# Joined products in two more gate units of the first attention and two more units of the second

## The reference

```python
def first_block(x, ...):
    xn = rmsnorm(x, norm_attn[l])
    proj = xn @ w_in[l]
    rq, rk, rv, rg, sq, sk, sv, ga, gb = jnp.split(proj, split_points, axis=-1)
    ...                                             # retention over rq, rk, rv
    ret = ret.astype(x.dtype) * jax.nn.silu(rg)
    y_a = ret @ w_branch_ret[l]
    ...                                             # stick-breaking attention over sq, sk, sv
    y_b = sb @ w_branch_sb[l]
    mixed = jax.nn.sigmoid(ga) * y_a + jax.nn.sigmoid(gb) * y_b
    x = x + mixed @ w_out[l]
    ...                                             # experts: every one of 16384, gated by a top 16

def second_block(x, ...):
    xn = rmsnorm_2(h, norm1_g[layer])
    proj = xn @ w_in[layer]
    q_a, k_a, v_a, q_r, f_r, i_r, g_r = jnp.split(proj, IN_SPLITS, axis=-1)
    attn = moba_attention(q_a, k_a, v_a)            # at 256 tokens: causal softmax with a distance term
    rec = hgrn2(q_r, f_r, i_r, g_r, lb_all[layer], rec_norm_g[layer])
    h = h + jnp.concatenate([attn, rec], axis=-1) @ w_out[layer]
    ...                                             # experts again
```

## Time and profile before

| | us |
|---|---|
| median of 3 runs | 1983.34 (1983.23 to 1983.45) |
| profiled execution, its own time | 1983.32 |
| its span | 1981.5 |
| PE busy | 1973.2 |
| DVE, ACT, POOL busy | 1282.0, 1043.9, 1424.8 |

### The profile page before, as it was taken

How to read it: one execution, slowest core, us unless ns; L and a number is a source line. 1 busy time by engine, 2 the same in 40 slices (tenths; PEclk the granted TensorE clock), 3 DMA queues, 4 the chain that set the end, 5 groups by cost and what they waited for, 6 DMA issues and landing times.

```text
span 1981.5 us, 38996 instructions
## 1 busy us (share of the span) xinstructions
PE 1973.2 (100%) x13942; PEld 1763.5 (89%) x13942; DVE 1282.0 (65%) x2183; ACT 1043.9 (53%) x1364; POOL 1424.8 (72%) x604
## 2 busy tenths in 40 slices
PE   9999999999999999999999999999999999999998
PEld 8899898888888888888889899888888888888887
DVE  5256387864776899953336748886467789994333
ACT  6556555565555544445447665556555554444444
POOL 7667878888777878854448757888877787884442
PEclk9999999999999999999999999999999999999999
DMA  8444545555555555566555345555555555555553
GB/s 271 163 139 149 178 162 186 189 183 189 179 170 174 176 169 171 174 209 206 194 188 180 124 143 170 191 188 185 181 178 169 174 176 170 175 174 180 201 191 127
DMA packets 100467, 351.44 MB, mean 177 GB/s; under 512 B 12464, under 2 KB 15408, under 8 KB 100272
## 3 DMA queue, kind: packets, MB, share of 16 engines
q1 hardware_dynamic: 99680, 348.61, 52.9%
q10 hardware_dynamic: 720, 1.92, 0.3%
HBM read 349.44 MB, written 1.05 MB: 177 GB/s over the span
## 4 chain that ended last, share of the span: by engine, by line
PE 99%; DMA 0%; DVE 0%; ACT 0%; POOL 0%; SPq 0%; issue 0%
PE ps L1268 24%; PE ps L1334 12%; PE ps L1269 12%; PE ps L1336 12%; PE ps L1337 6%; PE ps L1335 6%; PE ps L739 4%; PE ps L741 4%; PE ps L740 4%; PE ps L896 4%; PE ps L1260 3%; PE ps L898 2%; PE ps L933 1%; PE ps L823 1%; PE ps L1244 1%; PE ps L1146 1%
## 5 line engine op out<-in xcount | busy, mean ns | idle before, releaser
L657 POOL TENSOR_TENSOR wlo<-ring,whi 128x1024 fp32r<-128x1024 f32 x565 | 1370.3, 2431 | 515.0 <-ACT whi L1694 427.7
L1694 ACT ACTIVATE whi<-ring 128x1024 fp32r<-128x1024 f32 x536 | 566.6, 1060 | 718.2 <-PE ps L1337 387.2
L1268 PE MATMUL ps<-hboth,whi 128*128 128x512 f32 x2048 | 714.6, 395 | 0.0
L1269 PE MATMUL ps<-hboth,wlo 128*128 128x256 f32 x2048 | 567.7, 277 | 0.0
L1268 PEld LDWEIGHTS ps<-hboth,whi 128*128 128x128 f32 x2048 | 384.1, 188 | 87.3
L1334 PE MATMUL ps<-whi,shi 128*128 128x512 f32 x1024 | 404.2, 395 | 0.0
L1336 PE MATMUL ps<-wlo,shi 128*128 128x512 f32 x1024 | 400.4, 391 | 0.0
L1269 PEld LDWEIGHTS ps<-hboth,wlo 128*128 128x128 f32 x2048 | 384.6, 188 | 0.0
L1337 PE MATMUL ps<-whi,slo 128*128 128x256 f32 x1024 | 286.7, 280 | 0.0
L1335 PE MATMUL ps<-whi,slo 128*128 128x256 f32 x1024 | 285.7, 279 | 0.0
L1336 PEld LDWEIGHTS ps<-wlo,shi 128*128 128x128 f32 x1024 | 192.2, 188 | 43.4
(11 more groups left out here) (335 smaller groups left out, 2893.7 us busy)
## 6 DMA issues: line engine op xcount, KB each, us to landing
ring<-in_weights SPq DMA_DIRECT2D x651, 512.0 KB, 3.3
act<-in_const SPq DMA_DIRECT2D x11, 198.0 KB, 3.5
act<-in_const SPq DMA_DIRECT2D x8, 192.0 KB, 4.9
xres<-in_x SPq DMA_DIRECT2D x4, 256.0 KB, 5.2
act<-in_keys ACTq DMA_DIRECT2D x1, 1024.0 KB, 4.7
ring<-in_weights SPq DMA_DIRECT2D x2, 256.0 KB, 5.0
act<-in_fgain ACTq DMA_DIRECT2D x1, 512.0 KB, 3.5
out<-act SPq DMA_DIRECT2D x1, 512.0 KB, 2.6
```

Source lines behind the costliest of these rows:

```text
L657: pool.tensor_tensor(wlo[:, j, :], ring[:, j, :], whi[:, j, :].bitcast(F32), ALU.subtract)\
L1268: pe.matmul(bank(b), whi[:, j, c], hboth[:, :, kc, :], start=kc == 0, stop=False, skip_group_check=True)
L1269: mm = pe.matmul(bank(b, 0, S), wlo[:, j, c], hhi[:, kc, :], start=False, stop=kc == KC - 1, skip_group_check=True)
L1694: eng.activation(whi[:, j, :], ring[:, j, :], ACT.Copy).then_inc(hi_ready[j], 1)
```

## The change

Four units change from `columns` to `joined_columns`: units 24 and 25 of the first attention (the last half of ga) and units 4 and 5 of the second (the first halves of qa and ka). Units 24 and 25 now use banks 2, 3 and 0, 1. Before these are written PE waits until the stick-breaking steps have read them (`stay_ready`, `arg_ready`). Units 4 and 5 use banks 4, 5 and 0, 1. The slots, the transfers and POOL's work stay as they are.

```diff
+JOINED_GATE_BANK = {24: 2, 25: 0}
...
-JOINED2_BANK = {1: 6, 2: 4, 3: 6}
+JOINED2_BANK = {1: 6, 2: 4, 3: 6, 4: 4, 5: 0}
...
+        gate_part = tmpA[:, :, 0:S]
...
-            def joined_columns(i, b, free, left=None):
+            def joined_columns(i, b, free, left=None, parts=(0, 1)):
...
-                for half in range(HALVES):
+                for half in parts:
...
+                        elif i in JOINED_GATE_BANK:
+                            free = (stay_ready, PAIRS) if i == 24 else (arg_ready, PAIRS)
+                            joined_columns(HALVES * i, JOINED_GATE_BANK[i], [free] * TT, parts=parts)
...
+                        if i in JOINED_GATE_BANK:
+                            b = JOINED_GATE_BANK[i]
+                            if i > 24:
+                                eng.wait_ge(gate_joined, i - 24)
+                            eng.activation(gate_part, ps[:, b:b + 2, S:2 * S], ACT.Copy).then_inc(gate_parted, 1)
...
-                        eng.wait_ge(slot_used, HALVES * (i + 1))
-                        eng.tensor_tensor(gateT[name][:, off // P:off // P + 2, :], bank(4 + i % 2).rearrange("p (j t) -> p j t", j=2),
-                                          R, ALU.mult).then_inc(gate_scaled, 1)
+                        if i in JOINED_GATE_BANK:
+                            b = JOINED_GATE_BANK[i]
+                            product = ps[:, b:b + 2, 0:S]
+                            eng.wait_ge(gate_parted, i - 23)
+                            eng.tensor_tensor(product, product, gate_part, ALU.add).then_inc(gate_joined, 1)
+                            eng.wait_ge(gate_joined, i - 23)
+                        else:
+                            product = bank(4 + i % 2).rearrange("p (j t) -> p j t", j=2)
+                            eng.wait_ge(slot_used, HALVES * (i + 1))
+                        eng.tensor_tensor(gateT[name][:, off // P:off // P + 2, :], product, R, ALU.mult).then_inc(gate_scaled, 1)
```

More of the change, by code:

```diff
@@ L478, in block_program @@
         so_copied = sem("sb_out_copied")
+        gate_parted = sem("gate_low_part_copied")
+        gate_joined = sem("gate_parts_joined")
         ret_parted = sem("ret_low_part_copied")
```

## The result

The changed kernel takes 1988.86 us in the median of 9 runs (1986.96 to 1990.8), the kernel before beside it 1983.23 (1982.95 to 1983.45): a ratio of 1.003, 95% interval 1.0022 to 1.0038. It is slower, by 5.6 us where 3.8 were forecast, and 0.06 us above the range. The changed kernel's runs spread over 3.8 us, those of before over 0.5.

A forecast was written before the change was run, and what follows sets the result against it. PE, busy 1973.2 of 1981.5 us, was taken to bound the kernel. 1983.32 + 2.53 (first attention's wait, net) + 1.2 (second's, net) = 1987.05, forecast 1987.1 us; range 1985.2 to 1988.8, over 8 in 10.

The forecast's parts named there:

- PE's saving: Joined matmuls in both attentions shorten PE's stream by 0.54 us in all, bounds 0.4 and 0.85.
- First wait: First attention, second branch unit: PE waits for unit 25's scaled product behind ACT's queue, +2.53 us net, bounds 2.3 to 2.9.
- Second wait: Second attention, first pair's transposes: PE waits for ACT's normalisation, delayed by copies and additions; +1.2 us net.
- The delay up to the maximum: Second attention's DVE and ACT chain: units 4 and 5 make it, through to the normalisation, 1.5 us later.
- 2.4 us to POOL before and 2.1 us now: Second attention: time three DVE differences and factors lose to POOL over SBUF, before and after the change.
- the bound of +2.0: Upper bound on the net cost at the second attention's first transposes; the lower bound was -0.35 us.
- Clock held: Forecast case: both waits appear and PE's clock does not fall; 60 in 100, own range 1986.2 to 1988.2 us.
- a rival of 12 in 100: Clock falls in the first attention's new wait, costing 1.7 us more: 1988.8 us; 12 in 100.
- the sign that I had given: Around the first attention's new wait, the granted clock should read 1.00 from 185 to 200 us.
- Rival 1: Both attentions: the hops are hidden and PE gains as the matmuls say, 1982.8 us; 5 in 100.
- Rival 2: Only the first attention's wait appears; the second chain keeps its room, 1985.5 us; 20 in 100.
- Rival 4: The four units are not actually joined; held excluded by PE's order, 64 rows shorter.

The follow-up runs named there:

- gates alone: Units 24 and 25 joined, units 4 and 5 of the second attention left plain, against the kernel before: 1987.06 us, ratio 1.0018.
- units 4 and 5 alone: Units 4 and 5 of the second attention joined, units 24 and 25 left plain, against the kernel before: 1984.93 us, ratio 1.0009.
- first wait moved: Changed kernel with branch units needing one gate unit less and unit 25's product awaited before the 16 transposes: 1985.22 us, ratio 1.0011 to the kernel before.
- the second time: The changed kernel measured again as it is, against the kernel before: 1989.46 us, ratio 1.0032.
- mended kernels: Changed kernel, unit 25's product awaited later, DVE taking units 4 and 5 behind a difference: 1983.55 us; with ga's Sigmoid also behind the turned heads' copies: 1983.05.
- All mended: Changed kernel with unit 25's wait, DVE's units 4 and 5 and ga's Sigmoid all moved later: ratio to the kernel before 0.9992, on another chip 0.9997 (1983.05 us).

## Why the forecast was wrong, point by point

- **PE's saving, 0.54 us.** The joined pieces lie 0.353 us apart in units 24 and 25 (180.66 to 185.96, 15 of them), as taken. In the second attention those of unit 5 lie 0.346 apart (1079.10 to 1083.95, 14 of them), and from the second branch unit to the start of unit 6 PE gains 0.32 us on the kernel before (1082.70 there, 1086.01 here, 3.31 against the shift of 3.63), where 0.34 was taken. So the rows bear the size out; with every wait gone the kernel's time is 0.2 to 0.6 us under before, which is within the noise.
- **First wait, +2.53 us net.** Right: 2.51 in the profiled execution, 2.45 and 2.52 in the runs of the gates alone. It was right because it followed ACT's queue, not the distance from PE to DVE: the engine named as the releaser, DVE, had been idle for 3.29 us.
- **Second wait, +1.2 us net.** The mechanism was right, the size 0.4 short (1.6). The delay up to the maximum, 1.5, was met with 1.53. The term that was mis-sized is what DVE loses to POOL, "2.4 us to POOL before and 2.1 us now": the three differences of 1084.07, 1091.63 and 1099.25 take 2.23, 2.00 and 2.23 us against 1.28 alone, and with factors that meet nobody the loss is 2.6 us. So the normalisation is 1.92 later and not 1.5. The result lies within the bound of +2.0.
- **"Clock held".** This is the step that failed: the forecast's sum has the clock at nothing. I had made the fall a rival of 12 in 100, for the first wait alone, on the ground that matmuls follow at once. They do follow, and the clock falls all the same, in the changed kernel's first profile 1.6 us after they have begun, and behind the second wait, where the sign that I had given (1.00 from 185 to 200) does not look. By the groups of runs it falls behind the wait of 2.5 us in 8 of 11 runs, and behind that of 1.8 us in 3 of 11 (units 4 and 5 alone) and 1 of 11 (first wait moved). By these shares, an estimate from other kernels on two chips, a run of the changed kernel has about 0.73 + 0.18 = 0.9 falls of 1.6 us, 1.45 us. With the second wait's size, 1987.05 + 0.4 + 1.45 = 1988.9; the median is 1988.86, and 1989.46 the second time, so that the agreement to 0.04 us is luck. The rival named its price well (1.7) and its odds badly, and the range's end of 1988.8 was its sum with one fall and a second wait of 1.2; with the 1.6 that was measured it would have been 1989.2, above the median.
- **Rival 1** (hops hidden) is refuted for this kernel, and is what the mended kernels come to, at 1983.05 where it said 1982.8. **Rival 2** (first wait only) is refuted by the second's 1.8 us. **Rival 4** by the 64 matmuls less.
- **The ramp** was not in the sum, rightly: it is no part of the change, but it stood with 1.1 us in one of the two profiles.

## What to carry to other kernels

When a product gets a second part that another engine must fold in, cost the hop by what stands in that engine's queue at the moment, and follow every result that waits behind it there, since the engine that the profile names as the releaser may have been idle. Where PE has no slack, count each new idle stretch of some 2 us or more twice: once for itself, and once more, weighted, for the clock that may fall after it. If a saving is half a microsecond, each new dependence must find its place before the joined product is worth anything, and then it is still hard to measure.

## What the runs showed of the hardware that I had not expected

- **The clock's fall can come when PE has long resumed.** In four profiles it began 0.5 us before PE resumed (gates alone) and 1.0, 1.3 and 1.6 us after that, and the granted clock then stood at the 1.2 GHz level for 3.4 us, in the midst of dense matmuls, at a price of 1.5 to 1.6 us. The same idle stretch in the same kernel has it in one execution and not in the next. With idle stretches of 1.3 us no run's time of 11 shows one.
- **DVE and POOL wait for each other's whole instruction.** A square of 0.68 us took 2.87 when POOL had begun 0.18 us earlier; a difference of 1.28 us took 2.23. Operations with one operand in PSUM were not held: DVE's addition and multiplication at 190.33 and 191.06 took 0.70 and 0.69 us while this row of POOL ran.

```profile
189.89 9.59 POOL L661 TENSOR_TENSOR wlo<-ring,whi 128x1024 fp32r<-128x1024 f32 x4 [5.01 <-ACT whi L1462]
```

  The Trainium skill ("GPSIMD Engine Reference", Specifications) names contention for instructions of VectorE with two SBUF inputs, and the rows agree on both sides.
- **The matmul stream isn't always equally fast.** On the chip where the kernel before took 1988 us the joined pieces of the first experts' stage lie further apart at a granted clock of 1.00. All mended there, and then on the other chip:

```profile
500.00:600.00 100.00, 100.00 (x777) 86.81 (x776) 69.40 (x99) 51.03 (x65) 77.58 (x34) 1.00 0.51 168
```
```profile
500.00:600.00 100.00, 100.00 (x787) 87.61 (x786) 70.83 (x100) 51.34 (x66) 79.65 (x34) 1.00 0.52 172
```

  10 matmuls fewer in 100 us, and nothing idle. From 444 to 675 us the pieces within a unit start 0.353 us apart instead of 0.347; ahead of this stretch and behind it both profiles have 0.347. The spans differ by 4.1 us. The chip alone isn't the cause, for five of the 26 runs there lie at 1983.9 to 1985.6, near the times of the other chips. Why is left open; it is a reason to compare kernels on one chip only, and to look at the single runs before two medians.
